# Half of a tile's first loads issued by ScalarE instead of SyncE, in a two-layer hybrid encoder

## What is computed

```python
for l in range(DEPTH):
    h = rmsnorm(x, attn_norm_g[l])
    proj = h @ w_in[l]
    q, k, v, conv_in, gate_logits = jnp.split(proj, SPLITS, axis=-1)
    ...
    ca, cb = jnp.split(conv_in, 2, axis=-1)
    u = ca * jax.nn.sigmoid(cb)
```

## Time and profile before

| | |
|---|---|
| median of 3 runs | 798.37 us (798.12 to 798.52) |
| the profiled execution | 798.24 us |
| its span | 796.4 us |
| TensorE matmul busy | 787.8 us (99%) |
| ScalarE busy | 547.5 us (69%) |
| VectorE busy | 520.3 us (65%) |
| GpSimd busy | 649.6 us (82%) |
| moved by DMA | 142.63 MB, mean 179 GB/s |

### The profile page before, as it was taken

The page is one execution under the profiler, slowest core; times in us unless marked ns, Lnnn a source line. Parts: engine busy times, 40 slices in busy tenths (PEclk is TensorE's granted clock), DMA queues, the critical chain, the costliest instruction groups (busy, mean ns, idle before and its releaser), DMA issues.

```text
span 796.4 us, 14013 instructions
## 1 busy us (share of the span) xinstructions
PE 787.8 (99%) x5470; PEld 718.0 (90%) x5470; DVE 520.3 (65%) x1186; ACT 547.5 (69%) x924; POOL 649.6 (82%) x182
## 2 busy tenths in 40 slices
PE   8999999999999999999999999999999999999997
PEld 8999989899988888888899999999899888888885
DVE  6899999674656666631359999885545666666101
ACT  7868978765676776763456577887546776767932
POOL 6999778787878888898869987878788888888982
PEclk9999999999999999999999999999999999999999
DMA  8655434444545555455454544434464555455631
GB/s 305 235 188 206 159 113 154 160 165 161 204 166 204 184 187 195 175 211 211 168 200 169 199 155 164 142 131 159 159 238 166 186 178 208 167 207 172 223 134 54
DMA packets 21378, 142.63 MB, mean 179 GB/s; under 512 B 2496, under 2 KB 3008, under 8 KB 4672
## 3 DMA queue, kind: packets, MB, share of 16 engines
q1 hardware_dynamic: 20736, 140.69, 49.9%
q10 hardware_dynamic: 576, 1.04, 0.4%
HBM read 140.68 MB, written 1.05 MB: 178 GB/s over the span
## 4 chain that ended last, share of the span: by engine, by line
PE 93%; DVE 3%; ACT 2%; DMA 1%; issue 0%; SPq 0%; DVEq 0%; ACTq 0%
PE four L1379 26%; PE four L1386 13%; PE four L1128 12%; PE four L1130 11%; PE four L1129 11%; PE four L1460 5%; PE four L1482 3%; PE four L1481 3%; PE four L1480 3%; PE four L1464 2%; DVE pc L817 2%; PE four L1262 1%; DMA x<-in_x_t 1%; PE ps L1240 1%; PE pt L1251 1%; ACT whi L345 1%
## 5 line engine op out<-in xcount | busy, mean ns | idle before, releaser
L288 POOL TENSOR_TENSOR wlo<-raw,whi 128x2048 fp32r<-128x2048 f32 x128 | 591.5, 4626 | 124.7 <-ACT whi L345 124.4
L345 ACT ACTIVATE whi<-raw 128x2048 fp32r<-128x2048 f32 x129 | 247.0, 1915 | 52.0 <-PE four L1464 27.4
L1379 PE MATMUL four<-u_both,whi 128*128 128x512 f32 x800 | 201.8, 392 | 0.0
L1128 PE MATMUL four<-h_both,whi 128*128 128x256 f32 x608 | 174.2, 286 | 0.0
L1130 PE MATMUL four<-h_both,wlo 128*128 128x256 f32 x608 | 172.0, 283 | 0.0
L1129 PE MATMUL four<-h_both,whi 128*128 128x256 f32 x608 | 172.0, 283 | 0.0
L1379 PEld LDWEIGHTS four<-u_both,whi 128*128 128x128 f32 x800 | 143.3, 189 | 25.1
L817 DVE SCALAR_TENSOR_TENSOR pc<-upad,par_all,pc 128x256 f32<-128x256 f32 x404 | 162.9, 481 | 0.1
L1128 PEld LDWEIGHTS four<-h_both,whi 128*128 128x128 f32 x608 | 116.5, 192 | 5.2 <-issue 5.2
L1386 PEld LDWEIGHTS four<-u_both,wlo 128*128 128x128 f32 x800 | 110.2, 190 | 8.6
L1129 PEld LDWEIGHTS four<-h_both,whi 128*128 128x128 f32 x608 | 116.6, 192 | 0.0
(11 more groups left out here) (278 smaller groups left out, 1242.8 us busy)
## 6 DMA issues: line engine op xcount, KB each, us to landing
raw<-in_weights SPq DMA_DIRECT2D x130, 1024.0 KB, 4.8
raw<-in_weights SPq DMA_DIRECT2D x3, 512.0 KB, 8.0
out_y<-qk SPq DMA_DIRECT2D x3, 256.0 KB, 2.4
x<-in_x_t SPq DMA_DIRECT2D x2, 256.0 KB, 3.9
raw<-in_weights SPq DMA_DIRECT2D x2, 256.0 KB, 3.9
x<-in_x_t SPq DMA_DIRECT2D x1, 512.0 KB, 6.9
gate<-in_final_g ACTq DMA_DIRECT2D x1, 512.0 KB, 3.7
out_y<-qk ACTq DMA_DIRECT2D x1, 256.0 KB, 3.0
```

Of the source, the lines that this page charges most:

```text
L288: nc.gpsimd.tensor_tensor(wlo[s][:, :], raw[s][:, :], whi[s][:, :].bitcast(f32), ALU.subtract).then_inc(lo_ready[s], 1)
L345: A(whi[s][:, :], raw[s][:, :], ACT.Copy).then_inc(hi_ready[s], 1)
L1128: MM(out, whi[s][:, w], hi, start=start, stop=False, skip_group_check=accumulate)
L1379: MM(to[:, m, :, :].rearrange("p a t -> p (a t)"), whi[u % RING][:, w], both[:, k, :, :].rearrange("p a t -> p (a t)"), start=(k == 0), st ...
```

## The change

Two calls of load_x leave SyncE's list, and two transfers of the same bytes with the same semaphores are issued by ScalarE behind its constants. SyncE keeps x tiles 0 and 1 and all weights.

```diff
@@ -252,9 +252,7 @@
             load_x(0, 1)
             load_pieces(0, 0, 1)
             load_pieces(0, 1, 2)
-            load_x(1, 2)
             load_pieces(0, 2, 4)
-            load_x(2, 4)
             load_pieces(1, 0, 2)
             load_pieces(1, 2, 4)
             sp.dma_start(pos_i, pos_in.partition_broadcast(P)).then_inc(pos_s, 16)
@@ -337,6 +335,8 @@
         def _(act):
             A = nc.scalar.activation
             act.dma_start(const[:, 0:NEARLY], const_in[:, 0:NEARLY]).then_inc(c_in, 16)
+            act.dma_start(x[:, 2:4, :], x_in[:, 2:4, :]).then_inc(x_in_s[1], 16)
+            act.dma_start(x[:, 4:8, :], x_in[:, 4:8, :]).then_inc(x_in_s[2], 16)
 
             def split_high(l, s, n):
 
```

## The result

The changed kernel takes 799.51 us (median of 22 runs, 798.63 to 800.71), the kernel before 798.45 us (22 runs, 798.03 to 798.99). The ratio is 1.0016, 95% interval 1.0010 to 1.0022: slower by 1.1 us, within the 0.2% that count as no change. The runs of the changed kernel lie in two groups, 13 at 798.6 to 799.6 and 9 at 800.2 to 800.7. The 22 runs of the kernel before have one group.

A forecast was written before the change was run, and what follows sets the result against it. TensorE's dense matmul stream was taken to bound the kernel, its restart gated by W23's landing. That landing moves from 8.73 to about 9.96; 1.23 - 0.13 = 1.1 us lost takes 798.37 to 799.5, range 797.9 to 800.6.

The forecast's parts named there:

- weights last: Main case at the start: the weights wait for x's bytes, time 799.0 to 800.1; chance 0.62.
- too little to be told: Whole-kernel outcome: a loss too small to tell from no change, about 0.2% or 1.6 us; chance 0.75.
- Issue work costs nothing: Kernel start: ScalarE's two extra issues and later table load stay under cover, 1.1 us of it left.
- The bytes are the limit, and x's bytes take from the weights: Start loads: engines already full, 2048 KB in at 10.0 either way; two queues only change who is last.
- the reading of two independent queues: Start loads: each issuing engine has its own queue, so W23 has 768 KB ahead and lands 0.7 us sooner.
- If both lines get equal shares: Start loads: SyncE's and ScalarE's lines share equally; W0 near 6.0, W1 7.4, X1 5.4, X2 8.3, W23 10.0.
- worst bound: Start loads: W23 lands last with a drawn-out tail, up to 0.8 us later, at 10.7.
- The real gate ... is the landing of W23: TensorE's restart at 11.95: set by W23 landing at 8.73, plus 1.15 us of ScalarE pieces and 0.9 of L402.
- in pieces of at most 0.7 us: TensorE between 8.9 and 13.1: idles in short pieces, 2.3 us in all, where it idled 0.9.
- the clock's case: Rival at TensorE's start: clock falls to 1.2 GHz, 2.5 us lost over 5 us, time 802.0; chance 0.03.
- The cap at 0.4 us by GpSimd: Fifth unit: GpSimd's low parts, ending 31.73 for TensorE's start at 32.03, limit any gain to 0.4 us.
- The loss persists to the end: TensorE's dense stream: a shift moves the kernel's end one for one; 1.1 us lost, none regained.

## Why the prediction came out

The forecast was 799.5 and the measured median is 799.51, in the range and in the case with most of the chance (0.62 for weights last, 0.75 for too little to be told). The direction and its ground were right. That the number came out to the digit is luck: a term was forecast at the wrong place, and a rival to which 0.03 was given occurred, by the runs' clocks, in 9 of 22 runs. A median between two groups lies where their sizes put it: here near the upper end of the lower group, whose own median is 799.27, while that of the upper group is 800.46.

- *Issue work costs nothing*: right. ScalarE's table load ran from 2.15 to 3.43 and ScalarE was idle until 4.62; the run with W0 and W1 as one transfer has both issues on ScalarE and lost nothing, and the one with X2 in two parts has three.
- *The bytes are the limit, and x's bytes take from the weights*: right, and against the reading of two independent queues; the rule of the Trainium skill that was weighed there (DMA: Bandwidth & Descriptors, "Issuing engines are not separate DMA queues") agrees with the trace: W1's time to landing went from 4.0 to 6.8 us. Nor did the second queue by itself move more: from 2 to 9 us the profiles with all of x on SyncE moved 2.09 to 2.26 MB, that of the changed kernel 2.24.
- *"If both lines get equal shares"*: **this step failed.** It gave W1 at 7.4 and X2 at 8.3. Measured were 8.4 and 9.2. The shares were equal in rows, not in bytes: 183 and 180 packets, but 0.45 and 0.33 MB from 4 to 6 us. With rows of equal length W1 landed at 7.3, near the forecast value. Shares are not all of it. By them X2 should be earlier than forecast, and nearly all of its bytes were (by 8.0), but its last packets came late. W1 too landed later than the count of bytes: by 7.0 SyncE's queue had moved 0.85 MB, X0, W0 and W1 together are 0.79, and W1 landed at 8.4. For W1 the prediction put such a tail at nothing; it had one for W23 alone, as its worst bound.
- *"The real gate ... is the landing of W23"*: right for the kernel before, wrong for the changed one. W23 came at 10.3 (10.0 forecast), but ScalarE was busy until 10.45, because W1 held up everything behind it. The second part, whose 9.5 was said to cost nothing, started at 10.59 and ended too late for the third. The loss without the clock was forecast at 1.1; the profile with five extra matmuls shows 1.5, and the 13 runs of the lower group have a median of 799.27, 0.8 above the kernel before. W1's landing, at 7.7 to 8.6 in the four profiles with these queues and rows, scatters that much. The warm-ups, taken at their length of before, also ended earlier: the first real matmul came at 6.35 instead of 6.97, which bought nothing and made the idle piece longer.
- *Idle "in pieces of at most 0.7 us"*: wrong, by the same step. The wait for the second part was 2.2 us in one piece, and so the clock's case was priced as rare. Its rate, half a microsecond per microsecond, gives 1.7 for the 3.4 us at 1.2 GHz. The rows give 1.5 (four matmuls started every 0.85 us instead of 0.48), and about 0.8 to 1.0 of it reached the end, since TensorE would have had waits of its own in that stretch. The rule cited for that rival (the Trainium skill, TensorE: Matmul & The Clock Gate, "Part 1: The HAM clock gate") agrees with the trace in what it says: the array fell to 1.2 GHz behind idleness.
- *The cap at 0.4 us by GpSimd*: right that GpSimd's low parts of the fifth unit are the cap, and about right in size: no version gained more than 0.46. Its chain was put down to V01 alone, though. With ScalarE's list in another order it hung on W23's pieces, and there TensorE's third part started half a microsecond earlier for 0.3 us of gain at most, once for a loss of 0.3.
- *The loss persists to the end*: right. TensorE was 2.5 us late at its fourth unit and 2.5 us late at its last matmul.

What stays open: why the transfers of one and the same list land up to 1.7 us apart from run to run (8.5 and 10.2 for W1 in the one-queue lists), and what exactly puts a run of the changed kernel into one or the other group. That the lower clock marks the upper group is seen in the run's own clocks (0.996 or 0.997 in all nine, 0.998 or 0.999 in the thirteen) and in the extra matmuls, with which it all but vanished. The kernel before has such a run too, one in its 103: 800.26 us at a mean clock of 0.996. But with X2 alone on ScalarE four of the eleven runs show 0.996 or 0.997 and are hardly slower than the others (799.63 to 799.93 beside 799.46 to 799.76); no profile shows one of them, and whether the clock fell at their start is not known. Two things could decide which group a run joins, and neither was tested: the scatter of W1, and the start of TensorE, whose same 26 warm-up instructions took from 4.7 to 5.9 us in the profiles.

## What to carry to other kernels

Moving loads to a second engine's queue added no bandwidth here, where the DMA engines were full; it changed who is last. So list the landings in the order in which they are needed, and look for the first consumer in a strictly ordered list, not for the one that the chain of waits happened to name. When two queues run side by side, compare the bytes per row of what stands in each: the queue with the longer rows got more bytes in every profile here, and merging the urgent transfers into one with longer rows undid the whole loss. A pipeline start with an idle piece of two microseconds on TensorE can be paid twice, as in the upper group here, once as the wait and once as the clock.

## What the runs showed of the hardware

**Two queues are served row by row.** In the part of the profile's page on DMA queues, q10 is ScalarE's. The constants, one later load of parameters, the final gain and one store give it 576 packets in the kernel before. With X2 (512 KB) on it, with X1 and X2, and with X1 and X2 in two parts, it has:

```profile
q10 hardware_dynamic: 720, 1.56, 0.6%
```

```profile
q10 hardware_dynamic: 864, 1.83, 0.6%
```

```profile
q10 hardware_dynamic: 1008, 1.83, 0.6%
```

Each transfer adds 144 packets, whether it is 256 or 512 KB: 128, one per partition, and 16 more. A packet of data is thus a partition's row, 2 or 4 KB. While both queues have work, the engines take as many packets from one as from the other: from 4 to 6 us 99 and 97, 183 and 180, 202 and 203, 140 and 141 in the four profiles above, whatever the rows' length. The Trainium skill (DMA: Bandwidth & Descriptors, "Queues, rings and completion order") says that an engine goes round the queues packet by packet. The counts agree, though what it calls a packet holds several descriptors, which no run here can show. They add that the rows' length decides who gets the bytes, 0.38 against 0.18 MB with rows of 4 and 2 KB. W1 landed at 8.4, 7.3 and 6.4 us where ScalarE's queue held rows of 2 and then 4 KB beside its 2, rows of 2 beside its 2, and rows of 2 beside its 4; each is one profile, and one list's W1 scatters by 0.9 us.

**The clock falls late and comes back.** In the changed kernel's profile TensorE idled from 8.4 to 10.6, ran at full clock until 12.4, but for another wait of 0.2, then at 1.2 GHz until 15.8, while it was working all the time. The fall comes after the idle piece has ended, and hits matmuls that nobody held up. In the run with X2 alone on ScalarE a wait of 1.7 us, right behind the warm-ups, left the clock at 1.00 in the profile until 794 us, and no execution took more than 799.93.
